# A one-layer encoder on one core: first gate groups without row dots, the residual added in quarters, terms loaded ahead of the last store, one gate block beside a memory head

## What is computed

```python
h = rmsnorm(x, g_mix)
gq, gk, gv, gr, ga, sq, sk, sv, mq, gates = split(h @ w_in)
y_gla, S  = gla(gq, gk, gv, gr, ga, state)           # 4 heads, blocks of 64 frames
y_swa     = sliding_window(sq, sk, sv, rel_table, sinks)
y_mem     = softmax(mq @ mk.T / 16) @ mv             # 4 heads, 256 memory tokens
g1, g2, g3 = split(sigmoid(gates))
x2 = x + (g1 * y_gla + g2 * y_swa + g3 * y_mem) @ w_out
q  = rmsnorm(rmsnorm(x2, g_ffn) @ w_peer_q, g_peer_q)
# each token: 8 heads x 16 experts of 128 x 128, chosen by two top-16 lists
y  = x2 + sum_e gate[t, e] * gelu(h2[t] . peer_u[e]) * peer_v[e]
out = rmsnorm(y, g_final)
```

## Time and profile before

| | |
|---|---|
| median of 3 runs | 4915.33 us |
| profiled execution: time | 4918.65 us |
| profiled execution: span | 4916.6 us |
| mean granted clock of TensorE | 0.994 |
| PE / DVE / POOL / ACT busy | 98 % / 66 % / 58 % / 30 % |
| DMA | 1013.06 MB, 206 GB/s on the mean |

### The profile page before, as it was taken

The page is one execution under the profiler, slowest core; times in us unless marked ns, Lnnn a source line. Parts: engine busy times, 40 slices in busy tenths (PEclk is TensorE's granted clock), DMA queues, the critical chain, the costliest instruction groups (busy, mean ns, idle before and its releaser), DMA issues.

```text
span 4916.6 us, 78844 instructions
## 1 busy us (share of the span) xinstructions
PE 4838.2 (98%) x32224; PEld 4723.2 (96%) x32224; DVE 3264.3 (66%) x4242; ACT 1497.5 (30%) x2899; POOL 2844.3 (58%) x1650
## 2 busy tenths in 40 slices
PE   8999999999999999999999999999999999999998
PEld 8999999999998879998999999999999999999998
DVE  5877777774423534217577777666666899999855
ACT  5333333332423432102312126666662000000001
POOL 7200000003333435555277879998997999999976
PEclk9999999999999999999999999999999999999999
DMA  7334334335343536523444449999998888888852
GB/s 275 116 126 131 126 127 128 124 127 149 107 155 127 205 131 229 186 91 128 131 141 141 141 157 333 337 335 336 335 333 295 302 315 305 305 313 302 314 181 104
DMA packets 343207, 1013.06 MB, mean 206 GB/s; under 512 B 39728, under 2 KB 132112, under 8 KB 307232
## 3 DMA queue, kind: packets, MB, share of 16 engines
q1 hardware_dynamic: 165776, 526.23, 32.0%
q0 software_dynamic: 36864, 268.45, 14.5%
q10 hardware_dynamic: 140208, 213.34, 12.1%
HBM read 882.26 MB, written 126.76 MB: 205 GB/s over the span
## 4 chain that ended last, share of the span: by engine, by line
PE 91%; DVE 4%; DMA 2%; ACT 1%; POOL 1%; issue 1%; ACTq 0%; POOLq 0%; DVEq 0%; SPq 0%
PE ps L248 21%; PE ps L252 21%; PE ps L250 21%; PE ps L761 7%; PE ps L762 7%; PE ps L760 7%; PE ps L2821 1%; PE ps L1153 1%; PE ps L1593 1%; PE ps L1170 1%; DMA ex_gate<-gate 0%; DVE in_sums L681 0%; PE ps L1559 0%; PE ps L2516 0%; PE ps L1856 0%
## 5 line engine op out<-in xcount | busy, mean ns | idle before, releaser
L218 POOL TENSOR_SCALAR w_hi<-w_raw 128x1024 fp32r<-128x1024 f32 x678 | 788.7, 1163 | 1908.5 <-PE ps L762 1079.7
L221 POOL TENSOR_TENSOR w_lo<-w_raw,w_hi 128x1024 fp32r<-128x1024 f32 x678 | 1695.8, 2501 | 56.5
L248 PE MATMUL ps<-h_hi,w_hi 128*128 128x416 f32 (+1 forms) x3552 | 1051.1, 330 | 1.0 <-ACT later_beside L410 1.0
L252 PE MATMUL ps<-h_hi,w_lo 128*128 128x416 f32 (+1 forms) x3552 | 1034.3, 326 | 0.0
L250 PE MATMUL ps<-h_lo,w_hi 128*128 128x416 f32 (+1 forms) x3552 | 1026.4, 323 | 0.0
L248 PE MATMUL ps<-ex_c_hi,w_hi 128*128 128x416 f32 x2048 | 719.4, 351 | 4.5 <-DVE ex_y L3121 2.5
L252 PE MATMUL ps<-ex_c_hi,w_lo 128*128 128x416 f32 x2048 | 723.8, 353 | 0.0
L250 PE MATMUL ps<-ex_c_lo,w_hi 128*128 128x416 f32 x2048 | 716.2, 350 | 0.0
L248 PEld LDWEIGHTS ps<-h_hi,w_hi 128*128 128x128 f32 x3552 | 622.8, 188 | 8.9 <-issue 4.8
L250 PEld LDWEIGHTS ps<-h_lo,w_hi 128*128 128x128 f32 x3552 | 622.2, 188 | 6.2
L252 PEld LDWEIGHTS ps<-h_hi,w_lo 128*128 128x128 f32 x3552 | 619.9, 188 | 2.4
(11 more groups left out here) (373 smaller groups left out, 9258.2 us busy)
## 6 DMA issues: line engine op xcount, KB each, us to landing
w_raw<-weights SPq DMA_DIRECT2D x906, 512.0 KB, 4.0
up<-up_out ACTq DMA_DIRECT2D x128, 208.0 KB, 6.6
gate<-g_sb_g ACTq DMA_DIRECT2D x13, 2048.0 KB, 13.4
proj<-rows_out ACTq DMA_DIRECT2D x97, 272.0 KB, 2.9
ex_up<-up ACTq DMA_DIRECT2D x16, 832.0 KB, 6.9
ex_gate<-gate ACTq DMA_DIRECT2D x16, 832.0 KB, 16.9
sp_first<-proj ACTq DMA_DIRECT2D x48, 272.0 KB, 3.6
sp_first<-up ACTq DMA_DIRECT2D x15, 832.0 KB, 7.2
```

The costliest lines, as they stand in the source:

```text
L218: pool.tensor_scalar(self.whi[:, to, :], self.raw[:, slot, :], 1.0, 1.0, ALU.mult, ALU.mult).then_inc(self.hi_done, 1)
L221: pool.tensor_tensor(self.wlo[:, to, :], self.raw[:, slot, :], self.whi[:, to, :].bitcast(F32), ALU.subtract).then_inc(self.split_done, 1)
L248: pe.matmul(acc, hi, x, start=first, stop=False)
L252: mm = pe.matmul(acc, lo, x, start=False, stop=last)
```

## The change

Six edits, from the first lines of the diff to the last.

1. LATER_MEM is 1 and MEM_SHARES is eight shares of 2 chunks: one gate block goes beside a memory head in place of two. LATER is 16, so PAIRS is 48: the four blocks go into two more Winograd pairs.
2. In stage_gla SP loads q and k ahead of v.
3. In stage_output_and_query ACT does a root of one column ahead of the squares.
4. In stage_gates DVE does no row dot in the first two groups.
5. In stage_experts y is not loaded with x2. Set 0's blocks are copied into y; x2 comes in quarters into one new tile `x_part`, and DVE adds each at the end of set 2, 4, 6 and 8. SP loads the next quarter when the add before has been made (`x_added`); pieces stand behind that wait.
6. In stage_experts ACT loads the terms of set 1 when the gate table is stored, and waits for the stores of the up blocks after that.

```diff
@@ -80,8 +80,8 @@
...
 
-LATER_START, LATER_SWA, LATER_MEM = 4, 2, 2
-SWA_SHARES, MEM_SHARES = (3, 3, 2, 3, 3, 2), (4, 4, 4, 4)
+LATER_START, LATER_SWA, LATER_MEM = 4, 2, 1
+SWA_SHARES, MEM_SHARES = (3, 3, 2, 3, 3, 2), (2,) * 8
 LATER = LATER_START + LATER_SWA * SWA_KV + LATER_MEM * MEM_HEADS
@@ -1026,13 +1026,13 @@
...
                 if needed(h):
-                    sp.wait_ge(pe_s.sem, pe_s.at(f"v{NP}", before))
-                sp.dma_start(v[:, :, :], some(B_GV, VC, h)).then_inc(v_loaded, 16)
-                if needed(h):
                     sp.wait_ge(dve_s.sem, dve_s.at("k_even", before))
...
                 sp.dma_start(k[:, :, :], some(B_GK, KC, h)).then_inc(qk_loaded, 16)
+                if needed(h):
+                    sp.wait_ge(pe_s.sem, pe_s.at(f"v{NP}", before))
+                sp.dma_start(v[:, :, :], some(B_GV, VC, h)).then_inc(v_loaded, 16)
                 if needed(h):
@@ -1859,7 +1859,7 @@
...
                 of_block = len(MEM_SHARES)
-                later.share(pe, beside(h) + p // of_block, (p // of_block) % 2, MEM_SHARES, p % of_block)
+                later.share(pe, beside(h) + p // of_block, (beside(h) + p // of_block) % 2, MEM_SHARES, p % of_block)
 
@@ -2289,6 +2289,7 @@
...
             act.wait_ge(*ended["vector"])
+            act.activation(norm.std[:, 0:1], core.eps, ACT.Sqrt)
             for k in range(KD):
@@ -2758,6 +2759,7 @@
...
     evict_after = [EVICT_AFTER_FIRST] + pe_after[1:]
+    DOTS_FROM = 2
     DOTS_AFTER = [1, 1, 1, 2, 1, 1, 1, 2]
@@ -2847,7 +2849,7 @@
...
                                       at.unsqueeze(2).to_broadcast([P, GROUP, N_KEYS]), ALU.is_equal).then_inc(hot, 1)
-                for _ in range(DOTS_AFTER[group % STEPS]):
+                for _ in range(DOTS_AFTER[group % STEPS] if group >= DOTS_FROM else 0):
                     if s < SLOTS:
@@ -2939,7 +2941,9 @@
...
         rstd = core.acc_view(1)
-        y_loaded = [sem(f"y_loaded{n}") for n in range(4)]
+
+        x_part, x_part_loaded, x_added = sb("x_part", [P, 4, T]), sem("x_part_loaded"), sem("x_added")
+        x_set = lambda n: 2 + 2 * n
         terms_loaded = [sem(f"terms_loaded{s}") for s in range(2)]
@@ -2954,12 +2958,14 @@
...
         def _(sp):
-            sp.wait_ge(*ended["tensor"])
+            at = AT_DOWN + RING
             for n in range(4):
-                sp.dma_start(y[:, 4 * n:4 * n + 4, :], rows("x2")[:, 4 * n:4 * n + 4, :]).then_inc(y_loaded[n], 16)
-                if n < AHEAD:
-                    core.load_piece(sp, (AT_DOWN + n) % RING, AT_DOWN + RING + n)
-            core.load_pieces(sp, AT_DOWN + RING + AHEAD, N_PIECES)
+                core.load_pieces(sp, at, down_at(x_set(n) - 1) + RING)
+                at = down_at(x_set(n) - 1) + RING
+                if n:
+                    sp.wait_ge(x_added, 2 * n)
+                sp.dma_start(x_part[:, :, :], rows("x2")[:, 4 * n:4 * n + 4, :]).then_inc(x_part_loaded, 16)
+            core.load_pieces(sp, at, N_PIECES)
             for first, end in ((0, 3), (3, POOL_SCALED)):
@@ -3051,8 +3057,9 @@
...
                         act.wait_ge(sparse.gates_stored[parity], 16 * ((G_TILES + 1 - parity) // 2))
+                    load_terms(1)
+                    for parity in range(2):
                         act.wait_ge(up_blocks.stored[parity], 16 * (N_KEYS // 2))
-                    load_terms(1)
                     act.wait_ge(sparse.dotted, SLOTS)
@@ -3114,12 +3121,14 @@
...
                         dve.wait_ge(core.piece_used, down_at(G) + j // 2 + 1)
-                    if needed(G):
+                    if G == 0:
+                        dve.tensor_copy(y[:, j, 0:TD], ps[:, 4 + j % 4, 0:TD]).then_inc(added, 1)
+                    else:
                         dve.wait_ge(added, KD * (G - 1) + j + 1)
-                    elif j % 4 == 0:
-                        dve.wait_ge(y_loaded[j // 4], 16)
-                    dve.tensor_tensor(y[:, j, 0:TD], ps[:, 4 + j % 4, 0:TD], y[:, j, 0:TD],
-                                      ALU.add).then_inc(added, 1)
+                        if G == x_set(j // 4) + 1:
+                            dve.wait_ge(x_added, 2 * (j // 4) + 2)
+                        dve.tensor_tensor(y[:, j, 0:TD], ps[:, 4 + j % 4, 0:TD], y[:, j, 0:TD],
+                                          ALU.add).then_inc(added, 1)
                     if G < LAST:
@@ -3134,7 +3143,15 @@
...
                         s += 1
+                for n in range(4):
+                    if G == x_set(n):
+                        at = slice(4 * n, 4 * n + 4)
+                        dve.wait_ge(x_part_loaded, 16 * (n + 1))
+                        dve.wait_ge(added, KD * (G + 1))
+                        dve.tensor_tensor(y[:, at, 0:TD], y[:, at, 0:TD], x_part[:, :, 0:TD], ALU.add).then_inc(x_added, 1)
+                        dve.tensor_copy(y[:, at, TD:T], x_part[:, :, TD:T]).then_inc(x_added, 1)
                 if G == SPARSE_SETS + 1:
+                    dve.wait_ge(x_added, 8)
                     dve.wait_ge(summed_or_turned, 1)
```

## The result

The changed kernel takes 4920.58 us (median of 17 runs, 4915.9 to 4998.93; the highest is one execution at a mean clock of 0.918, left out of the ratio), the kernel before 4913.03 (17 runs). The ratio is 1.0015 with a 95 % interval of 1.0008 to 1.0022: 7.5 us slower, by medians; that is small, but the interval lies above 1. Forecast were 4902 us and a gain; the time lies outside the range of 4889 to 4913, and the change slows the kernel where a gain was forecast. The profiled execution took 4923.83 us, its span is 4922.0, 5.4 us more than that of before.

The account below looks back on a forecast made before the run. PE bounds the kernel, busy 4838.2 of 4916.6 us. Terms -6.0 + 4.1 - 4.0 + 0 - 8.6 + 1.0 = -13.5 take 4918.65 to 4905.2 profiled, 3.3 less as median: 4902 us, range 4889 to 4913.

Parts of the forecast that it names:

- rival D: Memory heads become bound by the softmax, 20 tile steps each 1.5 us short plus half clock: +30 and more, 4935; chance 0.04.
- the wait at L1122 and its slow stretch: GLA stage before the change: PE waits 1.8 us, then 10 us at half clock; used to price clock loss after waits.
- the 1.5 of clock: stage_gla: 1.5 us lost at low clock behind PE's wait for v; gate stage: 1.5 us regained at the eighth product.
- the 5.4: Gate stage, L2821: PE's 5.4 us wait at the gate products, forecast to go away.
- rival E: stage_output_and_query: the table load's drain is on the path, so the forecast moves by 2.7 us to 4899; chance 0.04.
- Edit 5a: Expert stage start: set 1's terms loaded without waiting for the last up store; -8.6 us, bounds -8.6 and -6.
- Edit 5b: Expert stage: x2 added in quarters at the ends of sets 2, 4, 6, 8; +1 us, bounds 0 and +15.
- SP's hold: Expert stage: x_part's load waits for DVE's add, pieces behind it; fifth piece split 1.5 us early, three times.
- Rival C: Gain given back by queues: SP's three holds cost 3 to 4 us each or POOL's second gate-stage wait is full; 4913, 0.22.

## Why the prediction was wrong

**What bounds, and the size of the steps ahead of the experts: right in sum, wrong in part.** I had -6.0 + 4.1 - 4.0 + 0 = -5.9 us up to the expert stage; the shift there is -8.2. That the two are so near is luck: 6.4 us at L1122 that I had not forecast make up for the 3.8 by which edit 3 fell short and for 2.9 lost at low clocks.
- Edit 1: -6.0 forecast for the pairs, -6.1 measured, and no wait in the memory heads; rival D is out. What I did not see is that the wait at L1122 and its slow stretch, which I read as a thing of the GLA stage and used only as a price, would go with it, after 1.5 us lost at a low clock behind stage_memory.
- Edit 2: +2.6 of wait forecast, 2.08 measured, the 1.5 of clock did not come.
- Edit 3: the mechanism was right, the waits of PE for the split came as laid out (3.3 and 3 us forecast, 3.35 and 2.53 measured) and the 5.4 went. The net was -4.0 forecast and -0.2 measured (-8.0 to -8.2 in the table). The term was mis-sized by what the layout left out: the clock behind the first new wait, windows of 0.83 at 2935 to 2945 with 10 and 32 matmuls (1.7 us, an estimate from the two), a third wait for the split of 0.5, and one of 1.6 at the gate products behind the one that had waited 5.4. So that product came 0.7 us earlier, not 2.5; the 1.5 of clock behind it did come, and the 1.6 took them back.
- Edit 4: 0 forecast. The root now has no load before it:

```profile
2229.51 0.71 ACT L312 ACTIVATE oq_std<-ps,const_sb 128x544 f32<-128x544 f32 x1 [2.13 <-PE ps L2253]
```

but PE's wait behind it is 6.75 us in both kernels, since the root starts 1.1 us after the first of PE's sums in both. The drain that the Trainium skill states behind the load ("ScalarE: Activation LUTs", What ACT_TABLE_LOAD costs) is nowhere on the path here: the root is 9.4 us earlier, as everything ahead of it, so the edit gave nothing, and rival E is out. Behind PE's wait 1.4 us of the lead are lost in the changed kernel, at clocks of 0.50 and 0.80 from 2235 to 2245. They are lost in 5 of the 12 profiled kernels with this edit and not in the other 7; what decides it is open.

**Edit 5a: the size about right, the reason wrong.** -8.6 forecast, -7.3 measured at the stage's start (shift -8.2 to -15.5). It came from x2's load being away, not from the order of terms and stores, so that the size came out is luck: with x2 there the order gave 2 us, without it nothing.

**Edit 5b: the step that failed.** I took +1 us, bounds 0 to +15; it was +20.3. The failing part is SP's hold. Two sizes in it were too small. The add and copy took 6.05 us at the end of set 2 and 6.1 at that of set 6, not 2.3 (3.4 at the end of sets 4 and 8, where the copy took 0.4): I scaled a row of 2048 elements and chose the near end, though the row beside it, 1.94 us for 416 columns, pointed to the far one. So SP was let go 6.9 us into set 3, where I had 2.6 to 5.6. The piece behind the quarter took 9.3 us to land, not 7.0. With these the piece is split 2.3 us late where I had it 1.5 early, and the sign that I had set for being wrong, a wait for `w_lo` over 2 us, came in sets 3 and 7. Then I priced the three places as independent, while by the rows above each makes the next worse by way of the gathers on POOL, and left the clock out again: in set 7 a wait of 4.46 us costs 7.8. The upper bound, three times 5, held neither of these.

The Trainium skill's sentence on GpSimd's interface ("GPSIMD Engine Reference", Specifications) spoke for the long end, and the runs agree: beside the add and the copy one subtraction of POOL takes 3.92 us where others take 2.4 to 2.6, and 1664 columns took DVE 2.94 to 3.52 us in the changed kernel where the earlier trace rows scaled gives 1.9 (with the quarters four pieces later two of the four adds did take 1.9). I had quoted it, and not moved the number.

Rival C was the one that came, with its place right (SP's holds), and it went beyond what I had given it: 11 us for all queues, 4913, where SP's holds alone took 20.3.

## What to carry to other kernels

A load that waits for its consumer must not stand in the queue that feeds everything else, unless the pieces loaded ahead of it cover the consumer's worst time; placing it two pieces later, or a second tile, gave some 17 us back here. When an engine is busy over 90 %, price what is added by the slow row, and ask what the engines behind it do when it is late: here a late engine that frees buffers for others came back on itself. And when several edits touch one stretch, a gain that is seen there belongs to none of them until one is taken away alone.

## What was not expected of the hardware

- A wait of PE is not followed by the same clock each time. Behind 2.31 us in set 3 the clock stayed at 1.00, behind 1.96 in set 5 it was 0.66 in the next five microseconds (17 matmuls for 28), behind 4.46 in set 7 0.83 for ten. What decides it is open.
- Between 1500 and 1510 the clock fell in all 13 profiled kernels with edit 1 (windows of 0.56 to 0.79), where no wait of PE is shown ahead of it and the kernel before has 1.00; this took 1.5 us back in twelve and 3.1 in one. What brings it is open.
- The first load of ex_gate, with the 4.4 MB of x2 in the queues, took 21.3 us to land before the change and about 25 with x2 loaded ahead again, and 10.1 to 10.8 without.
- The copy of 128x512 took 2.6 us where a subtraction of POOL ran beside it and ended with it, to within 0.3 us, and 0.41 at the ends of sets 4 and 8, where POOL was issuing a gather.
